# One quarter of the conditioning moved out of the first attention into the first projection, and the second gate's sums gathered inside the down stage

## The reference, cut to what matters

```
mod = silu(c) @ w_ada + b_ada                  # 2048 -> 6 * 2048
shift1, scale1, gate1, shift2, scale2, gate2 = split(mod, 6)
h = rms(x, norm1_w) * (1 + scale1) + shift1
u, q, k, v = split(h @ w_in)                   # 2048 -> 4096
y_ssm = s5_mixer(u, ...)                       # scan over the tokens, then @ w_glu
y_att = dilated_attention(q, k, v)             # 8 heads of 128
x = x + gate1 * (concat(y_ssm, y_att) @ w_out)
h2 = rms(x, norm2_w) * (1 + scale2) + shift2
x = x + gate2 * ((silu(h2 @ w_gate) * (h2 @ w_up)) @ w_down)
... second block: swiglu, pooling and causal attention, swiglu
```

## Time and profile before

| | us |
|---|---|
| median of 3 runs | 3419.1 (3419.04 to 3423.09) |
| profiled execution, its own time | 3418.91 |
| its span in the trace | 3416.8 |
| TensorE busy | 3190.7 (93%) |
| VectorE busy | 1925.2 (56%) |
| ScalarE busy | 1209.9 (35%) |

### The profile page before, as it was taken

How to read it: one execution, slowest core, us unless ns; L and a number is a source line. 1 busy time by engine, 2 the same in 40 slices (tenths; PEclk the granted TensorE clock), 3 DMA queues, 4 the chain that set the end, 5 groups by cost and what they waited for, 6 DMA issues and landing times. The chain is left out here.

```text
span 3416.8 us, 57672 instructions
## 1 busy us (share of the span) xinstructions
PE 3190.7 (93%) x25282; PEld 3105.7 (91%) x25282; DVE 1925.2 (56%) x1800; ACT 1209.9 (35%) x1067; POOL 198.0 (6%) x194
## 2 busy tenths in 40 slices
PE   3499758799999999999999999999899999999999
PEld 3499648799999999999999999999659999999999
DVE  7888597867444444654445445654335554455454
ACT  2264423333233333433333333433324433333333
POOL 3434120000000000000000000021000000000000
PEclk6699859899999999999999999999859999999999
DMA  9765357577555555555555555588205555555553
GB/s 328 243 204 191 129 185 271 210 270 268 174 185 185 188 189 187 185 170 177 173 173 172 178 175 176 173 173 171 79 1 178 181 187 188 182 191 187 185 184 136
DMA packets 328689, 630.26 MB, mean 184 GB/s; under 512 B 22452, under 2 KB 24008, under 8 KB 328280
## 3 DMA queue, kind: packets, MB, share of 16 engines
q1 hardware_dynamic: 317512, 624.79, 55.6%
q10 hardware_dynamic: 11040, 3.51, 0.5%
HBM read 626.16 MB, written 2.10 MB: 184 GB/s over the span
## 5 line engine op out<-in xcount | busy, mean ns | idle before, releaser
L409 DVE TENSOR_TENSOR w_lo<-raw,w_hi 128x2048 fp32r<-128x2048 f32 x496 | 1139.6, 2298 | 1266.7 <-ACT w_hi L404 1266.5
L404 ACT ACTIVATE w_hi<-raw 128x2048 fp32r<-128x2048 f32 x496 | 949.8, 1915 | 1803.5 <-PE ps L542 1755.1
L540 PE MATMUL ps<-act_hi,w_hi 128*128 128x256 f32 (+1 forms) x5056 | 1440.4, 285 | 48.8 <-DVE w_lo L409 28.8
L541 PE MATMUL ps<-act_lo,w_hi 128*128 128x256 f32 (+1 forms) x5056 | 1438.8, 285 | 0.0
L542 PE MATMUL ps<-act_hi,w_lo 128*128 128x256 f32 (+1 forms) x5056 | 1436.5, 284 | 0.0
L540 PEld LDWEIGHTS ps<-act_hi,w_hi 128*128 128x128 f32 x5056 | 959.1, 190 | 52.6 <-issue 26.4
L541 PEld LDWEIGHTS ps<-act_lo,w_hi 128*128 128x128 f32 x5056 | 958.2, 190 | 0.1
L542 PEld LDWEIGHTS ps<-act_hi,w_lo 128*128 128x128 f32 x5056 | 957.7, 189 | 0.0
L540 PE MATMUL ps<-hid_hi,w_hi 128*128 128x256 f32 (+1 forms) x2880 | 814.8, 283 | 12.7 <-DVE w_lo L409 8.2
L542 PE MATMUL ps<-hid_hi,w_lo 128*128 128x256 f32 (+1 forms) x2880 | 812.9, 282 | 0.0
L541 PE MATMUL ps<-hid_lo,w_hi 128*128 128x256 f32 (+1 forms) x2816 | 795.5, 283 | 0.0
(11 more groups left out here) (285 smaller groups left out, 1607.8 us busy)
## 6 DMA issues: line engine op xcount, KB each, us to landing
raw<-in_w_ada SPq DMA_DIRECT2D x96, 1024.0 KB, 5.1
raw<-in_ffn_w_gate SPq DMA_DIRECT2D x88, 1024.0 KB, 5.0
raw<-in_ffn_w_up SPq DMA_DIRECT2D x88, 1024.0 KB, 5.0
raw<-in_ffn_w_down SPq DMA_DIRECT2D x88, 1024.0 KB, 5.0
raw<-in_w_in SPq DMA_DIRECT2D x64, 1024.0 KB, 5.9
raw<-in_w_ffn_gate SPq DMA_DIRECT2D x44, 1024.0 KB, 5.1
raw<-in_w_ffn_up SPq DMA_DIRECT2D x44, 1024.0 KB, 5.1
raw<-in_w_ffn_down SPq DMA_DIRECT2D x44, 1024.0 KB, 5.0
```

Source lines behind the costliest of these rows:

```text
L404: act.activation(w_hi[b][:, :, :], raw[j % RING][:, :, :], ACT.Copy).then_inc(hi_ready, 1)
L409: dve.tensor_tensor(w_lo[b][:, :, :], raw[j % RING][:, :, :], w_hi[b][:, :, :].bitcast(F32), ALU.subtract).then_inc(lo_ready, 1)
L540: pe.matmul(o, whi, hi[:, k, cols], start=(k == 0 and not (shared and m % 2)), stop=False)
L541: pe.matmul(o, whi, lo[:, k, cols], start=False, stop=False)
```

## The change

- `w_in` becomes four turns of (SV)x8: 32 S and 32 V chunks, a V after every S. Its V chunks now carry gate1 and shift2. `GATE1_AT` has seven gathers in place of three, and both parts go into `mod` with one addition of 32 columns after the last.
- The phase `attn` is gone, with its sums `accs2`, its gathers and the three small VectorE steps at the attention's end. SP fetches the `glu` chunks ahead there.
- `w_out` carries scale2 in place of shift2; `gain` is made from it ahead of the second norm, in three linked VectorE steps in place of one.
- The gate2 sums are gathered by TensorE before chunk 2 of `down0`, into bank 4, and it waits for VectorE's reading before chunk 4. VectorE reads them before it splits chunk 3. The first turn of `down0` is written out on TensorE to hold this.

```
-    add("w_in", 4, 2, 4, "SSVSSVSSVSSV")
-    add("attn", 1, 0, 4, "V" * 16)
+    add("w_in", 4, 2, 4, "SV" * 8)
...
-        GATE1_AT = (10, 19, 28)
+        GATE1_AT = (7, 10, 13, 16, 22, 25, 28)
...
         def gate2_pe(pe):
             p = byname["ffn1.up0"]
-            pe.wait_ge(bank_free[0], group_index(byname["ffn1.down0"], 0, 0))
+            pe.wait_ge(bank_free[1], group_index(byname["ffn1.down0"], 0, 1))
             for g in range(4):
                 pe.wait_ge(acc_step, CK * (p.before["V"] + 4 * g + 4))
-                gather(pe, accg2[:, g, :], 0, 4 * g)
+                gather(pe, accg2[:, g, :], 4, 4 * g)
+
+        def gate2_read(pe):
+
             pe.wait_ge(mod_read, 1)
...
-                if after_up:
-                    after_up(pe)
-                products(pe, f"{f}.down{i}", *hidden(f), cols, counted(hid_ready, hid0(byname[f"{f}.up{i}"])))
+                products(pe, f"{f}.down{i}", *hidden(f), cols, counted(hid_ready, hid0(byname[f"{f}.up{i}"])),
+                         within={2: lambda: gate2_pe(pe), 4: lambda: gate2_read(pe)} if f == "ffn1" and i == 0 else None)
...
-                units_dve(dve, 0, lambda s_: condition(dve, p, 0, s_, accs2[:, s_ // 4, :], s_ % 4) if s_ < p.body else None)
-                dve.wait_ge(mod_sum, 16)
-                link(dve, "dve", dve.tensor_tensor(mod[:, SCALE2:SCALE2 + 16], ps[:, 5, 0:16], bada[:, SCALE2:SCALE2 + 16], ALU.add))
-                link(dve, "dve", dve.tensor_scalar(gain[:, :], mod[:, SCALE2:SCALE2 + 16], 1.0, None, ALU.add))
-                link(dve, "dve", dve.tensor_tensor(gain[:, :], gain[:, :], vecs[:, V_N2:V_N2 + 16], ALU.mult))
+                units_dve(dve, 0)
...
-                units_pe(pe, 0, conditioning)
+                units_pe(pe, 0, nothing)
...
-                def shift2():
+                def scale2():
                     dve.wait_ge(mod_sum, 20)
-                    dve.tensor_tensor(mod[:, SHIFT2:SHIFT2 + 16], ps[:, 1, 0:16], bada[:, SHIFT2:SHIFT2 + 16], ALU.add)
+                    link(dve, "dve", dve.tensor_tensor(gain[:, :], ps[:, 1, 0:16], bada[:, SCALE2:SCALE2 + 16], ALU.add))
+                    link(dve, "dve", dve.tensor_scalar(gain[:, :], gain[:, :], 1.0, None, ALU.add))
+                    link(dve, "dve", dve.tensor_tensor(gain[:, :], gain[:, :], vecs[:, V_N2:V_N2 + 16], ALU.mult))
```

More of the change, by code:

```diff
@@ L513, in out_tile, with products @@
             return ps[:, 4 * half + m, 0:n]
-        def products(pe, name, hi, lo, cols, ready, norm=None, beside=None):
+        def products(pe, name, hi, lo, cols, ready, norm=None, beside=None, within=None):
             p = byname[name]
@@ L518, in products, with body @@
             shared = name == "w_in"
-            def body(it, norm=None):
+            def body(it, norm=None, within=None):
                 for j in range(p.per["S"]):
@@ L523, in body @@
                     half = g % 2
+                    if within and j in within:
+                        within[j]()
                     if norm and j == 3:
@@ L543, in body @@
                     mm.then_inc(chunk_done, 1)
-            if norm:
-                body(0, norm)
+            if norm or within:
+                body(0, norm, within)
             for it in range(p.iters if beside else 0):
                 body(it)
-            loop(pe, 1 if norm else p.iters if beside else 0, p.iters, body)
+            loop(pe, 1 if norm or within else p.iters if beside else 0, p.iters, body)
         linked = {"dve": 0, "act": 0, "pool": 0}
@@ L864, in settle @@
                     up()
-                    if p.name == "ffn1.down0":
-                        gate2_dve(dve)
                     if p.g0:
@@ L869, in settle @@
                             dve.wait_ge(bank_free[h], p.g0 // 2)
-                pending = run_phase(dve, f"{f}.down{i}", split_lo, bind(dve, last if i == len(PARTS) - 1 else evac), settle)
+                pending = run_phase(dve, f"{f}.down{i}", split_lo, bind(dve, last if i == len(PARTS) - 1 else evac), settle,
+                                    ahead={3: lambda: gate2_dve(dve)} if f == "ffn1" and i == 0 else None)
             return pending
@@ L1284, in _ @@
                 stream(sp, "w_in")
-                stream(sp, "attn", rest=False)
+                stream(sp, "glu", rest=False)
                 sp.wait_ge(x_in, 32)
@@ L1416, in _ @@
                 pe.wait_ge(y_ready, BLOCKS)
-                pe.wait_ge(acc_step, CK * (byname["w_in"].before["V"] + 16))
-                gather(pe, accg1[:, 1, :], 7, SEQ + 12)
+                pe.wait_ge(acc_step, CK * (byname["w_in"].before["V"] + 32))
+                gather(pe, accg1[:, 1, :], 7, SEQ + 28)
         def head_cols(b):
@@ L1713, in _ @@
                 v_pe(pe, 0)
-                def conditioning(s_):
-                    if s_ in (4, 8, 12, 16):
-                        g = s_ // 4 - 1
-                        pe.wait_ge(acc_step, CK * (byname["attn"].before["V"] + 4 * g + 4))
-                        gather(pe, accs2[:, g, :], 5, 4 * g)
-                units_pe(pe, 0, conditioning)
+                units_pe(pe, 0, nothing)
         y_lo = hid_hi[:, 8:16, :]
```

24 lines of the change are left out of this document (7 added, 17 removed).

## The result

The changed kernel takes 3379.42 us (median, 3375.84 to 3381.78) where the kernel before takes 3419.23 (3419.04 to 3423.09): a ratio of 0.9877, with a 95% interval from 0.9862 to 0.9892. The profiled execution took 3378.43, its span 3376.3, 40.5 less than before.

A forecast was written before the change was run, and what follows sets the result against it. TensorE was taken to bound the kernel and w_in, VectorE the first attention. Terms -32 (attention), +12 (w_in) and -6.4 (gate2 seam) sum to -26.4, from 3418.9 to 3392.5 us; range 3379 to 3409.

The forecast's parts named there:

- The attention, -32: First attention: with its two conditionings per pair of steps gone, 32 us saved in all (range 20 to 39).
- The pair at half clock, 6.8: First attention: two steps take 6.8 us at granted clock 0.50, derived from the second attention's pair; 3.4 a step.
- the low bound: First attention: least time of a pair, TensorE's busy time with no gap, 6.1 to 6.4 us, 3.1 a step.
- The clock, a chance of 0.05: First attention, rival: granted clock rises to 2.4 GHz, a pair takes about 5.0 us, 14 more saved, 3379; chance 0.05.
- The tail: First attention, from the last logits to its end, 10.1 us before: 4 us saved (3 to 5).
- w_in, +12: Phase w_in: the additional conditionings and gathers lengthen it by 12 us (low end +6.6, high end +21).
- VectorE becomes the bound here, +9.5: w_in, chunk 10 to 31: eleven more conditionings, 35.2 us against 25.7 of waits, add 9.5; four gathers hidden behind VectorE.
- The 0.9 for contention: w_in: 0.9 us added for more conditionings running beside GpSimd than the mean has.
- dearer in w_in: w_in, rival: half of VectorE's 25.7 us of waits cannot be filled, +10 to +13, total 3404; chance 0.12.
- The gate, -6.4: Seam after ffn1.up0: the wait behind the gate2 sums and the clock ramp go, 6.4 us saved (4.5 to 6.6).
- The 1.9 of the ramp: Start of down0 after the gate2 wait: clock ramp from 0.50 to 1.00 disappears, 1.9 us of the gate's saving.
- The second norm and w_out, 0: Second norm: two more small VectorE steps fit in a wait, 0, at most 0.4 us; w_out transfers unchanged, 0.

The follow-up runs named there:

- the kernel without the moved conditioning: Changed kernel with w_in as before (SSVSSVSSVSSV, 16 V chunks), shift2's conditioning left out of the computation: 3369.6 us, ratio 0.9851 to the kernel before.
- the padding: Changed kernel with one idle VectorE instruction (512 columns, 0.78 us) more in each of the first attention's sixteen steps: 3385.38 us, ratio 0.9901 to the kernel before.
- the five: Five executions with the changed kernel's attention code and no filling; the 15 steps took 39.6, 40.8, 41.6, 42.5 and 41.6 us.
- the filled versions: Changed kernel, or its variant with 28 conditionings in w_in and 4 behind, plus unread idle TensorE matmuls in or ahead of the first attention: 3368.32 to 3376.37 us.

## Why the prediction was right and wrong

**What bounds the kernel before: right.** VectorE was the attention's bound, TensorE w_in's, and the change acted only where it was expected to.

**The attention, -32: wrong, and this is the step that failed.** It measured -45.7 from the first logits on (-40.4 and -5.3), with 1.2 lost ahead of them; the kernel without the moved conditioning puts it at 45. The mechanism was right (TensorE's order decides at 0.50, shown by the padding), the term of the sum was mis-sized, in two parts:
- *The pair at half clock, 6.8.* It measured 5.9, in some executions 6.1. The 6.8 was the second attention's pair less what the first lacks, and the last item of that subtraction, 1.5 for the meta keys and the 16 columns, was a guess without a row; with 5.9 to 6.1 for the answer it had to be 2.2 to 2.4. Over 7.5 pairs the 0.9 are 6.8 us. Worse was the low bound, "TensorE's busy time with no gap, 6.1 to 6.4". The measured pair lies below it, so it was no bound. The rows of one pair's matmuls add up to 6.9 us in both kernels, but before they cover 6.39 and afterwards 5.85, because they overlap more where nothing waits in between. TensorE after, from 447.98:

```profile
447.98 1.22 PE L1535 MATMUL ps<-proj 128*128 128x256 f32 x2
449.00 0.63 PE L1558 MATMUL ps<-pt,vt 128*128 128x128 f32 x2
449.43 0.64 PE L1547 MATMUL ps<-const,pn 128*128 128x128 f32 x2
449.85 0.63 PE L1535 MATMUL ps<-proj 128*128 128x128 f32 x2
450.53 1.22 PE L1558 MATMUL ps<-pt,vt 128*128 128x128 f32 x4
```

  Of the four rows behind the first, three begin 0.2 before the one ahead of them ends. Where a matmul waits, this overlap with the one ahead is lost, and the busy time of the engine holds it.
- *The clock, a chance of 0.05 for "1.00 throughout" and nothing for "in part".* 7.5 pairs at 5.9 are 44.3 us; 39.6 were measured, so by this estimate full clock in part gave 4.7 more in this execution, and 1.8 to 4.7 in the five. My ground against it was one stretch, 20 us of the second attention at 0.50. That showed that 0.50 is possible at 94% busy, not that it is the rule.

The tail was 4 and measured 5.3. "1 given back" beside GpSimd can't be seen apart.

**w_in, +12: near in size, by steps that fit VectorE, but not by the bound it named.** It measured +11.4, 9.5 against the kernel without the moved conditioning, and +9.6 to +14.2 in the five executions of this code. VectorE's own steps came near: at chunk 10 it is 7.4 later, counted from its first split (209.17 less 126.75 against 202.12 less 127.12; the steps said 3.0 + 3.7); from chunk 10 to 31 it is 8.2 more (181.9 against 173.6; the step said 9.5); from the last split to the reading of the sums it is 4.3 less (the step said 5.1). The 0.9 for contention: a conditioning instruction took 813 ns in the mean in place of 797, which is 2 us over all, the VectorE work beside GpSimd having grown. But the step "VectorE becomes the bound here, +9.5", with four gathers hidden behind it, did not happen: from chunk 10 on TensorE waits for nothing in this trace, and the gathers lie open on it. What ended last was TensorE, through its later start (2.0 more of rest in all), its gathers (3.2) and, by estimate from what these two leave, some 5 us of lower clock, a term that my sum for `w_in` did not have. The two paths lie within a few us of each other (1.8 at the last chunk, and 2.3 of waits for `w_hi` left on VectorE), so that the sum of the one met the length of the other is in part luck. The rival "dearer in w_in" is out: of 35.8 us of waits 33.5 were filled.

**The gate, -6.4: right in size.** 6.4 by itself in the medians, and all from GLU start to the end is 7.0 shorter in the first profile, 6.1 in the second, 6.5 with the gate alone. The 4.50 of the wait are gone in each. The 1.9 of the ramp were reasoned from a clock of 1.00 through the seam, which the first of these three has; the two others have a fall behind the gather and are only 0.5 to 0.9 longer.

**The second norm and w_out, 0: right**, the wait shrank from 1.29 to 0.39.

**What was late next.** I named VectorE's 4.3 us and its handoffs as the floor at full clock and priced a pair at 5.0; it takes 4.3 with GpSimd at rest; the filled versions' pairs, at 1.00 or a little less, take 4.4 to 5.6 beside it.

**The range.** The terms' extremes reached 3380 (at the other end they add up to 3415, where I wrote 3414), and I left half of the clock case out. With its own evidence (one stretch for, no stretch against a partial rise) the case of a partly full clock, 3385 by my pair and 3379 by the measured one, should have had a fifth of the chance or more. The sum of the misses: 12.6 in the attention (45.7 less 1.2 less 32, and rounding), 1 in w_in, 0.6 from GLU start on, together the 14.

## What to carry to other kernels

A bound "from below" must come from a row that has no waits in it: sum the operations where they run back to back, or take the distance between equal operations, not the busy time of an engine that waits. If an edit takes an engine from half busy to nearly always busy, the clock of TensorE is one of the terms, with a partial rise as its form in all five executions here; price the pair at both levels. Work that fills waits is nearly free as long as the other engine is not made to wait; what it brings with it on that other engine is not: 12 additional conditionings cost w_in 3 to 4 us (7 in one execution), about what their three gathers take on TensorE, and 16 cost it 10 to 14, or 6 where the first stands behind the normed input. Before an engine at 98% is called the bound, look whether the other one waits for it.

## What the runs showed of the hardware

- **TensorE's granted clock moves between its two levels in executions of the same code.** The same attention had it at 0.50 for 30 us with TensorE busy 99% of the time in one execution, and for 12 us in another; in w_in it fell to 0.51 between 205 and 210 in the profile of the changed kernel, after 10 us in which TensorE had been busy in 7.58; with the first conditioning late it was busy in 7.62 of the same 10 us, and the clock stayed at 1.00. The length of w_in varied by 4.6 us in five executions of the changed kernel's code (273.3 to 277.9), and TensorE's busy time, for the same matmuls, by 4.7 (255.2 to 259.9): the shortest has the highest mean clock (0.96), the others 0.94 to 0.95. The fall in the profile of the changed kernel:

```profile
195.00:205.00 10.00, 7.58 (x63) 7.17 (x63) 9.81 (x16) 9.36 (x19) 0.00 (x0) 1.00 0.73 241
205.00:210.00 5.00, 5.00 (x29) 4.52 (x29) 4.86 (x8) 2.80 (x5) 0.00 (x0) 0.51 0.95 358
210.00:215.00 5.00, 5.00 (x38) 4.72 (x37) 4.93 (x7) 1.70 (x4) 3.00 (x5) 0.80 0.93 322
```

- **Unread matmuls can pay for themselves.** One more in each step of the attention cost nothing that can be measured; 30 ahead of it, most of them in a rest of 5 us, kept the clock at 1.00 there, and the stretch up to the first logits took 23.6 to 25.4 us in four executions, against 25.7 to 27.0 without them.
- **Open:** what makes the clock fall in a stretch where TensorE never rests.
